# One level of seven products (quarter sums) in most of a feed-forward's first product, on one Trainium2 core

## The chip, the core and the metric

The kernel runs on one core of a Trainium2 chip: TensorE (matmuls), VectorE (DVE), ScalarE (ACT), GpSimd (POOL) and the DMA queues, issued here by SyncE (SP). The metric is the device time of one execution in microseconds; lower is better.

## The reference, cut to what matters

Two transformer-like layers follow each other on 512 tokens of width 1024. The change touches the very last stage, the feed-forward of the second layer:

```python
def sqrelu_mlp(h, w1, w2):
    a = jax.nn.relu(h @ w1)        # h 512 x 1024, w1 1024 x 4096
    return (a * a) @ w2            # w2 4096 x 1024
...
x = x + g2 * sqrelu_mlp(hx2, w_mlp1[l], w_mlp2[l])
```

All operands are float32.

## The kernel before

Every float32 operand is split into a high part (a copy rounded to fp32r, by ACT) and a low part (the operand less its high part, by VectorE), and a product is the sum of three matmuls: high x high, high x low, low x high (`products`, L682).

The first product of the last feed-forward has 32 column blocks of 128 output columns (`MF` = 32, numbered from `M1_N`). A block's weights are 1024 x 128, held as 128 x 1024 in `RAW`, four slots loaded by SP; its high and low parts lie in `WH` and `WL`, two slots each. The transposed tokens are in `HH` and `HL`, 8 blocks of the inner dimension by 512 tokens. `column_block` (L692) runs 8 x 3 matmuls of 512 tokens into one bank of PSUM. Blocks 0 and 1 are done in token halves (`token_half`, L705), so that they can start before the last tokens are there. For each block ACT makes the high part (L1458) of the block two ahead, then a Relu out of PSUM into `CT` (L2115); VectorE makes the low part (L2145) and squares into `M1` (L2960). Blocks wait for each other by counting semaphores (`w_high`, `w_low`, `w_used`, `mlp_relu`, `mlp_out`); a load waits until the low part of its slot is made (L534). GpSimd has nothing to do in this stage.

The second product (`down`, from `M2_N`) takes the 32 blocks of `M1` as stationary operands against rows of `w_mlp2`, which VectorE first multiplies by a gate row (`gate`, L2151). It has the same pace: 24 matmuls of 512 for each block. In other stages GpSimd works at elementwise additions and products, where VectorE is busy too; those rows are used below.

Of the kernel before, what the change touches and what calls it, by code (L numbers as in the profile page):

```python
# [8 lines left out]
F32 = mybir.dt.float32  # L9
F32R = mybir.dt.float32r  # L10
# [5 lines left out]
P = 128  # L16
T = 512
# [132 lines left out]
M1_ = 4096  # L150

# [53 lines left out]
def program(nc, a, laid, cst, dft, gmod, gcum, gpad, gexp, moved, out):  # L205
# [9 lines left out]
    with ctx:  # L215
# [4 lines left out]

        def sem(name):
            if name not in S:
                S[name] = ctx.enter_context(nc.semaphore(name))
            return S[name]

# [18 lines left out]
        sb("arena_front", [P, 10240])  # L244
        FHW = sb("last_high", [P, 4, D], F32R)
        FLW = sb("last_low", [P, 4, D], F32R)
        sb("arena_middle", [P, 6144])
        XL = sb("context_low", [P, KD, CTX], F32R)
        sb("arena_rest", [P, ARENA - 26624])
# [264 lines left out]

        def each(v, n):

            return v.unsqueeze(1).to_broadcast([P, n, v.shape[1]])
# [10 lines left out]
        def _(sp):  # L528
# [134 lines left out]
            blocks(sp, MF, columns(M1_N, 0, mlp1_v))  # L663
            blocks(sp, MF, rows(M2_N, a["w_mlp2_2"][0]))
# [16 lines left out]
        def _(pe):  # L681
            def products(out_, wh, wl, xh, xl, start, stop):  # L682


                pe.matmul(out_, wh, xh, start=start, stop=False)  # L685
                pe.matmul(out_, wh, xl, start=False, stop=False)  # L686
                return pe.matmul(out_, wl, xh, start=False, stop=stop)  # L687
# [744 lines left out]
            def mlp(g, j):  # L1432
                pe.wait_ge(sem("mlp_out"), 4 * g + j + 1)
                column_block(g, M1_N + j, j, HH, HL)

            for j in range(2, 4):
                mlp(0, j)
            with pe.Fori(1, MF // 4) as g:
                for j in range(4):
                    mlp(g, j)  # L1440
            down(M2_N, M2_A, MF, lambda t, m: m.then_inc(sem("rows_done"), 1) if t == NT - 1 else None,
                 lambda t: pe.wait_ge(sem("mlp_relu"), MF - 2 if t == 0 else MF))
# [3 lines left out]
        def _(act):  # L1446
# [658 lines left out]
            def mlp(g, j):  # L2105
                last = isinstance(g, int) and g == MF // 4 - 1 and j == 3
                if last:
                    for i in range(2):
                        act.wait_ge(sem("mlp_out"), 4 + i + 1)
                        act_split(0, i, M2_A, M2_N, arena(M1_, MF, T))  # L2110
# [12 lines left out]
        def _(dve):  # L2123
# [824 lines left out]
            def mlp(g, j):  # L2948
                last = isinstance(g, int) and g == MF // 4 - 1
                if last and j == 1:  # L2950
                    dve.wait_ge(sem("wb_in"), 48)
                if last and j > 0:
                    gate(M2_N + j - 1, WB)
                if last and j == 3:
                    for i in range(2):
                        act_split(0, i, M2_A, M1)
# [219 lines left out]
```

## Time and profile before

| what | value |
|---|---|
| median of the runs (1599.33 to 1599.58) | 1599.55 us |
| span of the profiled execution | 1597.8 us |
| TensorE busy | 1578.1 us, 99% |
| VectorE busy | 960.2 us, 60% |
| ACT busy | 676.3 us, 42% |
| GpSimd busy | 170.3 us, 11% |

The page has the busy share of each engine and the chain that ended last; further views give the groups of instructions, who waited for whom, and instructions in order of time. Matmuls overlap each other in their durations, so their pace is read from start times.

### The profile page before, as it was taken

The page shows a single profiled execution, that of the slowest core. Times are in us where ns is not written, and L with a number is a line of the kernel's source. Part 1 is how long each engine was busy: PE and PEld are TensorE (multiplying, and loading weights), DVE is VectorE, ACT ScalarE, POOL GpSimd, SP SyncE. Part 2 cuts the span into 40 slices and gives each one's busy share as a digit, 9 for nine tenths or more (in the row PEclk, how much of TensorE's full clock was granted, in tenths as well). Part 3 has the DMA queues.
Part 4 walks back from the last instruction along what each step waited for, and adds up shares of the span by engine and source line. Part 5 has one row for each costly group of instructions (what it writes and reads, how often), then busy time and mean ns, then how long its engine had stood idle before and what let it go on. Part 6 is the DMA issues. An engine that isn't in the chain of part 4 may idle for free.

```text
span 1597.8 us, 21438 instructions
## 1 busy us (share of the span) xinstructions
PE 1578.1 (99%) x8269; PEld 1299.1 (81%) x8269; DVE 960.2 (60%) x1435; ACT 676.3 (42%) x1178; POOL 170.3 (11%) x191
## 2 busy tenths in 40 slices
PE   9999999999999999999999999999999999999998
PEld 7878878789887877788888788877888888888886
DVE  5688867947545877776435448655577433355554
ACT  5464466555334333344334354544444422332321
POOL 2012134601001000000001132320000000000000
PEclk9999999999999999999999999999999999999999
DMA  7365243311354886532323133221223233323222
GB/s 201 93 166 126 80 107 78 89 47 39 132 197 145 280 286 227 188 100 92 115 92 119 42 96 86 67 72 55 80 80 119 80 92 103 93 95 103 92 95 77
DMA packets 198569, 180.67 MB, mean 113 GB/s; under 512 B 6078, under 2 KB 178189, under 8 KB 195412
## 3 DMA queue, kind: packets, MB, share of 16 engines
q1 hardware_dynamic: 195056, 171.13, 35.0%
q10 hardware_dynamic: 2276, 6.95, 1.3%
q0 software_dynamic: 1152, 1.44, 0.5%
q8 instruction: 56, 0.92, 0.2%
q14 instruction: 29, 0.24, 0.0%
HBM read 175.15 MB, written 4.58 MB: 112 GB/s over the span
## 4 chain that ended last, share of the span: by engine, by line
PE 92%; DVE 4%; ACT 2%; issue 1%; DMA 0%; POOL 0%; ACTq 0%; DVEq 0%; POOLq 0%
PE acc L685 17%; PE acc L686 16%; PE acc L687 16%; PE acc L728 7%; PE acc L729 7%; PE acc L730 7%; PE acc L1233 2%; PE acc L743 2%; PE acc L741 2%; PE acc L1235 2%; PE acc L1234 2%; PE acc L742 2%; PE acc L1377 1%; PE acc L1361 1%; DVE w_low L2145 1%
## 5 line engine op out<-in xcount | busy, mean ns | idle before, releaser
L2145 DVE TENSOR_TENSOR w_low<-w_raw,w_high 128x1024 fp32r<-128x1024 f32 x230 | 284.6, 1239 | 486.3 <-ACT w_high L1458 485.8
L1458 ACT ACTIVATE w_high<-w_raw 128x1024 fp32r<-128x1024 f32 x224 | 237.4, 1060 | 618.8 <-PE acc L687 367.9
L685 PE MATMUL acc<-h_high,w_high 128*128 128x512 f32 (+1 forms) x1248 | 487.2, 390 | 4.6 <-DVE h_low L2179 1.6
L687 PE MATMUL acc<-h_high,w_low 128*128 128x512 f32 (+1 forms) x1248 | 479.4, 384 | 0.0
L686 PE MATMUL acc<-h_low,w_high 128*128 128x512 f32 (+1 forms) x1248 | 479.2, 384 | 0.0
L685 PEld LDWEIGHTS acc<-h_high,w_high 128*128 128x128 f32 x1248 | 234.6, 188 | 64.0 <-issue 15.3
L687 PEld LDWEIGHTS acc<-h_high,w_low 128*128 128x128 f32 x1248 | 234.5, 188 | 47.1
L686 PEld LDWEIGHTS acc<-h_low,w_high 128*128 128x128 f32 x1248 | 234.7, 188 | 45.0 <-issue 1.2
L728 PE MATMUL acc<-w_high,act_high 128*128 128x512 f32 x496 | 193.3, 390 | 0.9 <-DVE arena L2671 0.6
L730 PE MATMUL acc<-w_high,act_low 128*128 128x512 f32 x496 | 193.0, 389 | 0.0
L729 PE MATMUL acc<-w_low,act_high 128*128 128x512 f32 x496 | 193.0, 389 | 0.0
L728 PEld LDWEIGHTS acc<-w_high,act_high 128*128 128x128 f32 x496 | 93.1, 188 | 21.0 <-DVE arena L2671 1.0
L730 PEld LDWEIGHTS acc<-w_high,act_low 128*128 128x128 f32 x496 | 93.1, 188 | 19.5
L729 PEld LDWEIGHTS acc<-w_low,act_high 128*128 128x128 f32 x496 | 93.1, 188 | 19.1
L2270 DVE SCALAR_TENSOR_TENSOR arena<-acc,conv_params,arena 128x511 f32<-128x511 f32 (+2 forms) x108 | 80.6, 746 | 2.5
L2662 DVE SCALAR_TENSOR_TENSOR arena<-acc,params,arena 128x511 f32<-128x511 f32 x88 | 65.7, 746 | 1.5
L2159 DVE TENSOR_TENSOR act_low<-arena,act_high 128x512 fp32r<-128x512 f32 x78 | 53.0, 685 | 10.7 <-ACT act_high L1466 10.7
L1466 ACT ACTIVATE act_high<-arena 128x512 fp32r<-128x512 f32 x78 | 47.9, 621 | 22.9 <-PE acc L730 19.1
L2151 DVE TENSOR_TENSOR w_raw<-w_raw,arena 128x1024 f32<-128x1024 f32 x40 | 48.7, 1218 | 0.0
L2984 POOL TENSOR_SCALAR small<-small 128x1 f32<-128x1 f32 x17 | 4.1, 239 | 378.7 <-ACT arena L1485 378.7
L2021 ACT ACTIVATE arena<-acc,small 128x512 f32<-128x512 f32 x32 | 21.7, 685 | 49.0 <-DVE small L2830 49.0
L1233 PE MATMUL acc<-w_high,h_high 128*128 128x512 f32 x96 | 37.7, 392 | 1.6 <-DVE h_low L2205 1.1
(392 smaller groups left out, 1955.7 us busy)
## 6 DMA issues: line engine op xcount, KB each, us to landing
w_raw<-w_in SPq DMA_DIRECT2D x68, 512.0 KB, 4.0
w_raw<-w_mlp SPq DMA_DIRECT2D x64, 512.0 KB, 3.9
w_raw<-w_up SPq DMA_DIRECT2D x44, 512.0 KB, 4.0
arena<-w_ada SPq DMA_DIRECT2D x13, 1024.0 KB, 7.9
w_raw<-w_out SPq DMA_DIRECT2D x24, 512.0 KB, 3.2
early<-w_ada SPq DMA_DIRECT2D x11, 1024.0 KB, 6.0
w_raw<-w_down SPq DMA_DIRECT2D x22, 512.0 KB, 3.2
w_raw<-w_branch_gate SPq DMA_DIRECT2D x16, 512.0 KB, 4.1
```

What stands on the lines that cost most here:

```text
L685: pe.matmul(out_, wh, xh, start=start, stop=False)
L686: pe.matmul(out_, wh, xl, start=False, stop=False)
L687: return pe.matmul(out_, wl, xh, start=False, stop=stop)
L728: pe.matmul(o, AH[:, r, tc], WH[:, s, fc], start=k_is_0, stop=False)
L729: pe.matmul(o, AH[:, r, tc], WL[:, s, fc], start=False, stop=False)
L730: m = pe.matmul(o, AL[:, r, tc], WH[:, s, fc], start=False, stop=False)
L1233: pe.matmul(o, xh, WH[:, n % 2, wc], start=k == 0, stop=False)
L1458: f(WH[:, off % 2, :], RAW[:, off % 4, :], ACT.Copy).then_inc(sem("w_high"), 1)
L2145: tt(WL[:, off % 2, :], RAW[:, off % 4, :], WH[:, off % 2, :].bitcast(F32), ALU.subtract).then_inc(sem("w_low"), 1)
L2159: tt(AL[:, r, :], src[:, 4 * g + j, :], AH[:, r, :].bitcast(F32), ALU.subtract)\
L2270: stt(tap(n)[:, lag:T], PS[:, conv_bank(n), 0:T - lag], CW[:, at:at + 1], tap(n)[:, lag:T], ALU.mult, ALU.add).then_inc(sem("conv_step"), 1)
L2662: stt(o, PS[:, ffn_bank(q, j), 0:T - lag], w, o, ALU.mult, ALU.add).then_inc(sem("ffn_step"), 1)
```

## The change

`WHOLE` = 6 blocks keep the old form. The other 26 form 13 pairs, and each pair (256 output columns x 512 tokens, inner dimension 1024) is computed as a 2 x 2 by 2 x 2 block product with seven instead of eight products of halves (Winograd's form of Strassen's method). A pair's weights are four quarters of 128 x 512. GpSimd's `first_sums` adds quarters 0+2 and 3+2; VectorE's `second_sum` and `fourth_sum` give two more. Sums of the token quarters are made once (`token_sums`, `token_high`, `token_low`). Each of the seven parts is 4 x 3 matmuls of 256 tokens (`part` on TensorE); its high (`part_high`, ACT) and low (`part_low`, VectorE) are made five parts ahead into a ring of six places, four in `WH`/`WL` and two in `AH`/`AL`. The results are combined by one copy (`keep_first`, ACT) and five VectorE operations of 256 elements (`second_part` to `second_quarter`), followed by Relus on ACT. The squares of a pair are one GpSimd operation of 1024 elements. Before the pairs, blocks 0 to 5 now write the Relu directly into `M1`. The loads of the last pairs and of the second product's first four rows wait for counts of `part_low`. The names that begin with `st_` are semaphores of earlier stages used again (`since` adds their old final count). `TOK0`, `TOK12` and `SUM31` lie over memory of the arena that is free by then; `second_sum` and `fourth_sum` write over raw quarters.

```diff
@@ -148,6 +148,8 @@
 AG_, AP_, APT_ = F_, F_ + 3072, F_ + 5120
 MT_ = 6144
 M1_ = 4096
+WHOLE, PAIRS = 6, 13
+RAWT_, TOK_, SUM_ = M1_ + 20 * T, (20480, 23552, 25600), 27648
...
+        def first_of(p):
+            return M1_N + WHOLE + 2 * p
+        def quarters(p):
+            at = first_of(p) % 4 * 1024
+            return RAW[:, :, :].rearrange("p a b -> p (a b)")[:, at:at + 2048].rearrange("p (q c) -> p q c", c=512)
+        SUM31 = arena(SUM_, 2, 512)
+        def operand(p, i):
+            q = quarters(p)
+            return [q[:, 0, :], q[:, 2, :], SUM31[:, 0, :], SUM31[:, 1, :], q[:, 3, :], q[:, 1, :], q[:, 0, :]][i]
+        def ring(s):
+            at = (s + 5) % 6
+            if at < 4:
+                c = slice(at % 2 * 512, at % 2 * 512 + 512)
+                return WH[:, at // 2, c], WL[:, at // 2, c]
+            return AH[:, at - 4, :], AL[:, at - 4, :]
+        def raw_tokens(i):
+            return arena(RAWT_ + 1024 * i, 4, 256)
+        def tokens(i):
+            if i < 3:
+                both = TOK12[:, i - 1] if i else TOK0[:, :, :, :]
+                return both[:, 0], both[:, 1]
+            return HH[:, 0:4, 256:512], HL[:, 0:4, 256:512]
+        def moving(i):
+            if i in (0, 5, 6):
+                k, tc = slice(0, 4) if i == 0 else slice(4, 8), slice(256, 512) if i == 6 else slice(0, 256)
+                return HH[:, k, tc], HL[:, k, tc]
+            return tokens([1, 2, 0, 3][i - 1])
+        def region(p, i):
+            bank, half = [(0, 0), (1, 0), (2, 0), (3, 0), (1, 256), (0, 0), (3, 0)][i]
+            return PS[:, 4 * ((p + 1) % 2) + bank, half:half + 256]
+        V1, V2, V3 = PAR[:, 0:2, :].rearrange("p a b -> p (a b)"), C1[:, 0:256], C1[:, 256:512]
+        def pair_out(p, first, n):
+            at = M1_ + (WHOLE + 2 * p) * T + first
+            return A[:, at:at + n]
...
-            blocks(sp, MF, columns(M1_N, 0, mlp1_v))
-            blocks(sp, MF, rows(M2_N, a["w_mlp2_2"][0]))
+            for j in range(WHOLE + 4):
+                columns(M1_N, 0, mlp1_v)(j // 4, j % 4)
+            def load_late(n, read, src, shape):
+                sp.wait_ge(sem("st_low"), since("st_low", read))
+                dst = RAW[:, n % 4, :]
+                if shape is not None:
+                    dst = dst.rearrange("p (k c) -> p k c", c=shape)
+                sp.dma_start(dst, src).then_inc(sem(f"w_in{n % 4}"), 16)
+            for p in range(2, PAIRS):
+                for e in range(2):
+                    j = WHOLE + 2 * p + e
+                    load_late(M1_N + j, 7 * (p - 2) + [7, 5][e], mlp1_v[:, :, j * P:(j + 1) * P], P)
+            w_mlp2 = a["w_mlp2_2"][0].rearrange("(k p) n -> k p n", p=P)
+            for j in range(4):
+                load_late(M2_N + j, 7 * (PAIRS - 2 + j // 2) + [7, 5][j % 2], w_mlp2[j], None)
+            with sp.Fori(1, MF // 4) as g:
+                for j in range(4):
+                    rows(M2_N, a["w_mlp2_2"][0])(g, j)
...
+            def part(p, i):
+                s = 7 * p + i
+                pe.wait_ge(sem("st_low"), since("st_low", s + 1))
+                if i == 0 and p == 1:
+                    pe.wait_ge(sem("mlp_relu"), WHOLE)
+                elif i == 0 and p > 1:
+                    pe.wait_ge(sem("st_read"), since("st_read", 2 * p - 3))
+                    pe.wait_ge(sem("st_out"), since("st_out", 5 * (p - 1)))
+                if p == 0 and 0 < i < 5:
+                    pe.wait_ge(sem("st_token_low"), since("st_token_low", [2, 3, 3, 4][i - 1]))
+                if i == 4:
+                    pe.wait_ge(sem("st_out"), since("st_out", 5 * p + 1))
+                elif i == 5:
+                    pe.wait_ge(sem("st_kept"), since("st_kept", p + 1))
+                elif i == 6:
+                    pe.wait_ge(sem("st_out"), since("st_out", 5 * p + 3))
+                o, (wh, wl), (xh, xl) = region(p, i), ring(s), moving(i)
+                for k in range(4):
+                    c = slice(k * P, (k + 1) * P)
+                    m = products(o, wh[:, c], wl[:, c], xh[:, k, :], xl[:, k, :], k == 0 and i < 5, k == 3, skip=i > 4)
+                if s == 7 * PAIRS - 1:
+                    m.then_inc(sem("w_used"), 2 * PAIRS)
+                else:
+                    m.then_inc(sem("st_done"), 1)
+            for p in range(PAIRS):
+                for i in range(7):
+                    part(p, i)
+            def pairs_read(t):
...
+            def token_high(i):
+                act.wait_ge(sem("st_tokens"), since("st_tokens", max(3, i + 1)))
+                if i == 3:
+                    used(0, M1_N + WHOLE - 1)
+                f(tokens(i)[0], raw_tokens(i), ACT.Copy).then_inc(sem("st_token_high"), 1)
+            def part_high(s):
+                p, i = divmod(s, 7)
+                if i in (0, 5):
+                    act.wait_ge(sem(f"w_in{first_of(p) % 4}"), 16 * (first_of(p) // 4 + 1))
+                elif i == 4:
+                    act.wait_ge(sem(f"w_in{first_of(p) % 4 + 1}"), 16 * (first_of(p) // 4 + 1))
+                elif i == 1:
+                    act.wait_ge(sem("st_sums"), since("st_sums", 2 * p + 1))
+                elif i == 6:
+                    act.wait_ge(sem("st_sums"), since("st_sums", 2 * p + 2))
                 else:
-                    split(g, M1_N + j + 2)
-                used(g, M1_N + j)
-                act.wait_ge(sem("mlp_out"), 4 * g + j + 3)
-                f(CT[:, j % 2, :], PS[:, j, :], ACT.Relu).then_inc(sem("mlp_relu"), 1)
-
-            blocks(act, MF, mlp, whole=1)
-            split(0, M2_N + 1)
-            down(M2_N, M2_A, MF, arena(M1_, MF, T), lambda m: act.wait_ge(sem("mlp_out"), MF + 4))
+                    act.wait_ge(sem("st_first"), since("st_first", p + 1))
+                if s > 5:
+                    act.wait_ge(sem("st_done"), since("st_done", s - 5))
+                else:
+                    used(0, M1_N + [-1, 4, 4, 5, 5, -1][s])
+                f(ring(s)[0], operand(p, i), ACT.Copy).then_inc(sem("st_high"), 1)
+            def keep_first(p):
+                act.wait_ge(sem("st_done"), since("st_done", 7 * p + 1))
+                if p:
+                    act.wait_ge(sem("st_out"), since("st_out", 5 * p - 4))
+                f(V1, region(p, 0), ACT.Copy).then_inc(sem("st_kept"), 1)
+            def first_quarter(p):
+                act.wait_ge(sem("st_done"), since("st_done", 7 * p + 6))
+                f(pair_out(p, 0, 256), region(p, 0), ACT.Relu).then_inc(sem("st_read"), 1)
+            def other_quarters(p):
+                act.wait_ge(sem("st_out"), since("st_out", 5 * p + 5))
+                f(pair_out(p, 256, 768), pair_out(p, 256, 768), ACT.Relu).then_inc(sem("st_read"), 1)
...
+            for s in range(7 * PAIRS):
+                p, i = divmod(s, 7)
+                if s + 5 < 7 * PAIRS:
+                    part_high(s + 5)
+                if s + 5 == 7 * PAIRS - 1:
+                    act.sem_inc(sem("w_high"), 2 * PAIRS)
+                if i == 6:
+                    first_quarter(p)
+                if i == 1:
+                    keep_first(p)
+                    if p:
+                        other_quarters(p - 1)
+                if s == 7 * PAIRS - 4:
+                    for j in range(2):
+                        act.wait_ge(sem("mlp_out"), 4 + j + 1)
+                        f(AH[:, (M2_A + j) % 4, :], M1[:, j, :], ACT.Copy).then_inc(sem("a_high"), 1)
+                if s == 7 * PAIRS - 3:
+                    gated_high(0, 7 * PAIRS - 4)
+                if s == 7 * PAIRS - 1:
+                    gated_high(1, 7 * PAIRS - 2)
+            other_quarters(PAIRS - 1)
...
+            def second_sum(p):
+                q = quarters(p)
+                dve.wait_ge(sem("st_first"), since("st_first", p + 1))
+                tt(q[:, 2, :], SUM31[:, 1, :], q[:, 0, :], ALU.add).then_inc(sem("st_sums"), 1)
+            def fourth_sum(p):
+                q = quarters(p)
+                dve.wait_ge(sem("st_sums"), since("st_sums", 2 * p + 1))
+                tt(q[:, 0, :], q[:, 2, :], q[:, 1, :], ALU.add).then_inc(sem("st_sums"), 1)
+            def part_low(s):
+                dve.wait_ge(sem("st_high"), since("st_high", s + 1))
+                h, l = ring(s)
+                tt(l, operand(*divmod(s, 7)), h.bitcast(F32), ALU.subtract).then_inc(sem("st_low"), 1)
+            def second_part(p):
+                dve.wait_ge(sem("st_done"), since("st_done", 7 * p + 2))
+                dve.wait_ge(sem("st_kept"), since("st_kept", p + 1))
+                if p:
+                    dve.wait_ge(sem("st_out"), since("st_out", 5 * p))
+                tt(V2, region(p, 1), V1, ALU.subtract).then_inc(sem("st_out"), 1)
+            def third_part(p):
+                dve.wait_ge(sem("st_done"), since("st_done", 7 * p + 3))
+                dve.wait_ge(sem("st_out"), since("st_out", 5 * p + 1))
+                tt(V3, V2, region(p, 2), ALU.subtract).then_inc(sem("st_out"), 1)
+            def last_quarter(p):
+                dve.wait_ge(sem("st_done"), since("st_done", 7 * p + 4))
+                dve.wait_ge(sem("st_out"), since("st_out", 5 * p + 2))
+                tt(pair_out(p, 768, 256), V3, region(p, 3), ALU.subtract).then_inc(sem("st_out"), 1)
+            def third_quarter(p):
+                dve.wait_ge(sem("st_done"), since("st_done", 7 * p + 5))
+                tt(pair_out(p, 512, 256), V3, region(p, 4), ALU.subtract).then_inc(sem("st_out"), 1)
+            def second_quarter(p):
+                if p == PAIRS - 1:
+                    dve.wait_ge(sem("w_used"), M2_N + 2)
                 else:
-                    split(g, M1_N + j + 2)
-                dve.wait_ge(sem("mlp_relu"), 4 * g + j + 1)
-                tt(M1[:, 4 * g + j, :], CT[:, j % 2, :], CT[:, j % 2, :], ALU.mult)\
-                    .then_inc(sem("mlp_out"), 1)
-
-            blocks(dve, MF, mlp, whole=1)
+                    dve.wait_ge(sem("st_done"), since("st_done", 7 * p + 7))
+                tt(pair_out(p, 256, 256), region(p, 6), V2, ALU.subtract).then_inc(sem("st_out"), 1)
...
+            split(0, M1_N + 2)
+            split(0, M1_N + 3)
+            token_sums()
+            square(0)
+            split(0, M1_N + 4)
+            square(1)
+            for i in range(3):
+                token_low(i)
+            split(0, M1_N + 5)
+            square(2)
+            part_low(0)
+            second_sum(0)
+            square(3)
+            square(4)
+            part_low(1)
+            part_low(2)
+            square(5)
+            part_low(3)
+            token_low(3)
+            part_low(4)
+            fourth_sum(0)
+            dve.sem_inc(sem("w_low"), 2 * PAIRS)
+            for s in range(7 * PAIRS):
+                p, i = divmod(s, 7)
+                if i == 0 and p:
+                    second_quarter(p - 1)
+                if i > 1 and i < 6:
+                    [second_part, third_part, last_quarter, third_quarter][i - 2](p)
+                if s + 5 < 7 * PAIRS:
+                    part_low(s + 5)
+                if i == 1 and p + 1 < PAIRS:
+                    second_sum(p + 1)
+                if i == 6 and p + 1 < PAIRS:
+                    fourth_sum(p + 1)
+                if p == PAIRS - 1:
+                    if i == 2:
+                        dve.wait_ge(sem("wb_in"), 48)
+                        gate(M2_N, WB)
+                    elif i == 3:
+                        gate(M2_N + 1, WB)
+                    elif i == 4:
+                        for j in range(2):
+                            act_split(0, j, M2_A, M1)
+                    elif i == 5:
+                        split(0, M2_N)
+                    elif i == 6:
+                        gate(M2_N + 2, WB)
+            second_quarter(PAIRS - 1)
...
+            def first_sums(p):
+                q = quarters(p)
+                for e in range(2):
+                    pool.wait_ge(sem(f"w_in{first_of(p) % 4 + e}"), 16 * (first_of(p) // 4 + 1))
+                if p:
+                    pool.wait_ge(sem("st_low"), since("st_low", 7 * (p - 1) + 4))
+                pool.tensor_tensor(SUM31, q[:, 0:4:3, :], each(q[:, 2, :], 2), ALU.add).then_inc(sem("st_first"), 1)
+            def squares(p):
+                pool.wait_ge(sem("st_read"), since("st_read", 2 * p + 2))
+                o = pair_out(p, 0, 1024)
+                pool.tensor_tensor(o, o, o, ALU.mult).then_inc(sem("st_square"), 1)
+            first_sums(0)
+            first_sums(1)
+            for p in range(PAIRS):
+                if p + 2 < PAIRS:
+                    first_sums(p + 2)
+                squares(p)
```

`token_sums` on VectorE is four operations of 1024 elements with two SBUF inputs; the fourth waits for the second, the second for the first. `token_low(i)` is one of 1024. In `down`'s first block TensorE waits for the last pairs' reads of PSUM (`pairs_read`).

## Rows read from the trace of the kernel before

**Rows 1.** The page: span, busy time, chain that ended last by engine
```profile
span 1597.8 us, 21438 instructions
...
PE 1578.1 (99%) x8269; PEld 1299.1 (81%) x8269; DVE 960.2 (60%) x1435; ACT 676.3 (42%) x1178; POOL 170.3 (11%) x191
...
PE 92%; DVE 4%; ACT 2%; issue 1%; DMA 0%; POOL 0%; ACTq 0%; DVEq 0%; POOLq 0%
```
**Rows 2.** Waits, 1254 to 1418: waiter <- releaser: us in total, times, longest
```profile
ACT w_high L1458 <- PE acc L687: 114.4, 30, 4.0
DVE w_low L2145 <- ACT w_high L1458: 108.4, 31, 4.8
```
**Rows 3.** Stretch: us, busy (instructions) by engine, granted clock, DMA share, GB/s
```profile
1254.37:1417.60 163.23, 163.23 (x723) 135.19 (x721) 59.56 (x66) 47.40 (x62) 0.00 (x0) 1.00 0.34 100
```
**Rows 4.** Timeline of TensorE: start us, us, engine, line, out<-in; block 2, second product
```profile
1254.37 0.40 PE L685 MATMUL acc<-h_high,w_high 128*128 128x512 f32 x1
...
1417.60 0.39 PE L728 MATMUL acc<-w_high,act_high 128*128 128x512 f32 x1
```
**Rows 5.** Timeline of TensorE: a matmul of 256 columns, 66 before 1254.37
```profile
1246.45 0.28 PE L685 MATMUL acc<-h_high,w_high 128*128 128x256 f32 x1
```
**Rows 6.** Timeline of VectorE, queued operations; the last has an input in PSUM
```profile
1414.65 0.69 DVE L2960 TENSOR_TENSOR arena<-arena 128x512 f32<-128x512 f32 x1
1415.25 1.22 DVE L2151 TENSOR_TENSOR w_raw<-w_raw,arena 128x1024 f32<-128x1024 f32 x1
1416.39 1.29 DVE L2159 TENSOR_TENSOR act_low<-arena,act_high 128x512 fp32r<-128x512 f32 x2
...
1011.34 0.42 DVE L2787 TENSOR_TENSOR arena<-arena,acc 128x255 f32<-128x255 f32 x1
```
**Rows 7.** Groups by form, 1250 to 1598, of ACT: xcount, busy us, mean ns
```profile
L1458 ACT ACTIVATE w_high<-w_raw 128x1024 fp32r<-128x1024 f32 x58 | 61.5, 1060 | 218.6 <-PE acc L687 118.8 <-PE acc L730 99.9
...
L1466 ACT ACTIVATE act_high<-arena 128x512 fp32r<-128x512 f32 x32 | 19.7, 620 | 4.3 <-PE acc L730 4.3
```
**Rows 8.** Single lines of GpSimd: ns min/median/max
```profile
L3023 POOL TENSOR_TENSOR arena<-arena,early x4: 2399/2411/2415, 105.0 to 181.2; 128x1024 f32<-128x1024 f32 x4
...
L3027 POOL TENSOR_TENSOR arena<-arena,small x3: 1909/1912/2953, 107.4 to 154.6; 128x1024 f32<-128x1024 f32 x3
```
**Rows 9.** Timelines of GpSimd and VectorE together; L2671 is a form's ns min/median/max
```profile
251.50 1.27 POOL L3048 TENSOR_TENSOR early<-early,masks 128x512 f32<-128x512 f32 x1
252.35 1.51 DVE L2145 TENSOR_TENSOR w_low<-w_raw,w_high 128x1024 fp32r<-128x1024 f32 x1 [0.86 <-ACT w_high L1458]
252.74 2.02 POOL L3046 TENSOR_TENSOR early<-early,small 128x512 f32<-128x512 f32 x1
...
1011.29 2.50 POOL L3134 TENSOR_TENSOR arena<-masks,arena 128x256 f32<-128x256 f32 x3 [21.01 <-PE acc L1280]
1011.67 0.83 DVE L2793 TENSOR_TENSOR act_low<-arena,act_high 128x448 fp32r<-128x448 f32 x1
1013.10 1.17 DVE L2793 TENSOR_TENSOR act_low<-arena,act_high 128x448 fp32r<-128x448 f32 x1
...
L2671 DVE TENSOR_TENSOR arena<-arena x22: 616/618/620, 526.1 to 763.2; 128x448 f32<-128x448 f32 x22
...
143.32 1.23 DVE L2330 TENSOR_TENSOR arena<-acc,arena 128x1024 f32<-128x1024 f32 x1
143.36 1.91 POOL L3032 TENSOR_TENSOR arena<-arena,small 128x1024 f32<-128x1024 f32 x1 [16.15 <-PE acc L880]
```
**Rows 10.** Timeline of VectorE: low part of block 3
```profile
1255.67 1.23 DVE L2145 TENSOR_TENSOR w_low<-w_raw,w_high 128x1024 fp32r<-128x1024 f32 x1 [1.06 <-ACT w_high L1458]
```
**Rows 11.** DMA issues on the page: xcount, KB each, median us to landing
```profile
w_raw<-w_mlp SPq DMA_DIRECT2D x64, 512.0 KB, 3.9
...
arena<-w_ada SPq DMA_DIRECT2D x13, 1024.0 KB, 7.9
```
**Rows 12.** Waits of TensorE over the whole span, the longest
```profile
PE acc L685 <- DVE h_low L2179: 1.6, 1, 1.6
```

More of the change, by code:

```diff
@@ L224, in sem, with since @@
             return S[name]
+        def since(name, n):
+            return ended[name][1] + n
         WH = sb("w_high", [P, 2, 1024], F32R)
@@ L681, in _, with products @@
         def _(pe):
[L682 to L687, printed above, removed]
+            def products(out_, wh, wl, xh, xl, start, stop, skip=False):
+                pe.matmul(out_, wh, xh, start=start, stop=False, skip_group_check=skip)
+                pe.matmul(out_, wh, xl, start=False, stop=False, skip_group_check=skip)
+                return pe.matmul(out_, wl, xh, start=False, stop=stop, skip_group_check=skip)
             def split_ready(g, off):
@@ L1430, in _ @@
             token_half(M1_N + 1, 1, 1, range(KD)).then_inc(sem("w_used"), 1)
[L1432 to L1442, printed above, removed]
+            for j in range(2, WHOLE):
+                if j > 3:
+                    pe.wait_ge(sem("mlp_relu"), j - 3)
+                column_block(0, M1_N + j, j % 4, HH, HL)
@@ L2117, in _, with relu @@
[L2117 to L2119 removed]
+            M1 = arena(M1_, MF, T)
+            def relu(j):
+                used(0, M1_N + j)
+                f(M1[:, j, :], PS[:, j % 4, :], ACT.Relu).then_inc(sem("mlp_relu"), 1)
+            def token_high(i):
[3 more added lines that the diff above has]
+                f(tokens(i)[0], raw_tokens(i), ACT.Copy).then_inc(sem("st_token_high"), 1)
@@ new lines, in _, with gated_high @@
+            split(0, M1_N + 2)
+            relu(0)
+            split(0, M1_N + 3)
+            relu(1)
+            for i in range(3):
+                token_high(i)
+            split(0, M1_N + 4)
+            relu(2)
+            split(0, M1_N + 5)
+            part_high(0)
+            relu(3)
+            relu(4)
+            part_high(1)
+            part_high(2)
+            relu(5)
+            part_high(3)
+            token_high(3)
+            part_high(4)
+            def gated_high(j, done):
+                n = M2_N + j
+                act.wait_ge(sem("w_gated"), gated_before(0, n))
+                act.wait_ge(sem("st_done"), since("st_done", done))
+                f(WH[:, n % 2, :], RAW[:, n % 4, :], ACT.Copy).then_inc(sem("w_high"), 1)
@@ L2122, in _, with squared @@
+            other_quarters(PAIRS - 1)
+            def squared(m):
+                if m < WHOLE:
+                    act.wait_ge(sem("mlp_out"), 4 + m + 1)
+                else:
+                    act.wait_ge(sem("st_square"), since("st_square", (m - WHOLE) // 2 + 1))
+            down(M2_N, M2_A, MF, M1, squared)
         @block.vector
@@ new lines, in token_low @@
+            def token_low(i):
+                dve.wait_ge(sem("st_token_high"), since("st_token_high", i + 1))
+                h, l = tokens(i)
+                tt(l, raw_tokens(i), h.bitcast(F32), ALU.subtract).then_inc(sem("st_token_low"), 1)
+            def second_sum(p):
[6 more added lines that the diff above has]
+                tt(q[:, 0, :], q[:, 2, :], q[:, 1, :], ALU.add).then_inc(sem("st_sums"), 1)
@@ new lines, in _ @@
+            split(0, M1_N + 2)
+            split(0, M1_N + 3)
+            token_sums()
+            square(0)
+            split(0, M1_N + 4)
+            square(1)
+            for i in range(3):
+                token_low(i)
+            split(0, M1_N + 5)
+            square(2)
[8 more added lines that the diff above has]
+            token_low(3)
```

55 lines of the change are left out of this document (34 added, 21 removed).

## The prediction

> **What bounds the kernel now.** I read the page first: TensorE is busy for 99% of the span and makes 92% of the chain that ended last [rows 1]. A busy matmul engine is no proof by itself, so the second view is the list of waits for the stretch of the changed product: ACT waits 114 us for TensorE and VectorE 108 us for ACT, and no row has TensorE wait [rows 2]. The stretch table says the same: 163.23 us, TensorE busy in all of it at a granted clock of 1.00 (its upper level, 2.4 GHz), VectorE in 59.6 us, ACT in 47.4, GpSimd in none [rows 3]. Third, the pace of the matmuls by start times, since their durations overlap. The first of the 30 whole column blocks starts at 1254.37 and the second product at 1417.60 [rows 4]: 163.23 / (30 x 24) = 0.2267 us for a matmul of 512 columns. So this stage is set by the number of matmuls times their pace, and a change that issues less matmul work gains until another engine becomes the slowest. The profiled span is 1597.8 us; the median is 1599.55, so 1.75 us lie around the span.
>
> **TensorE's part of the change.** A pair of column blocks took 2 x 24 matmuls of 512 columns: 48 x 0.2267 = 10.88 us. It becomes 7 parts of 4 x 3 matmuls of 256 columns, 84 in all. That is 7/8 of the columns in 1.75 times the instructions, so the pace of the short ones matters. The trace has 96 of them, in the two token-halved blocks: from 1246.45 to 1254.37 there are 66 steps [rows 4, 5], 0.120 us each. A part takes 12 x 0.120 = 1.44 us, a pair 10.08. Gain: 0.80 us a pair, 13 pairs, **10.4 us**. Each short matmul costs 13 ns over 256/2.4; that fixed piece, paid 84 times for 48, takes back 0.48 of the 1.36 us that 1/8 of a pair is.
>
> **VectorE's part.** Before, a pair asked VectorE for two low parts of 128x1024 and two squares of 128x512. Starts of queued operations lie 1.14 us apart for 1024 elements; an operation of 512 takes 0.69 and the next follows 0.60 after its start; 255 elements with an input in PSUM are followed at 0.33 [rows 6, 9]. Before: 2 x 1.14 + 2 x 0.60 = 3.5 us of each 10.88. After, for a pair: seven `part_low` and two sums (`second_sum`, `fourth_sum`), nine operations of 512 elements with both inputs in SBUF, 9 x 0.60 = 5.45; and five combinations of 256 with one input in PSUM, 5 x 0.34 = 1.70. **7.15 us**, which fits under 10.08. The squares go to GpSimd. ACT gets seven highs (0.62 at 512 elements), one copy and two Relus (each at most the 1.06 of 1024 elements) [rows 7]: at most 7.5 us a pair, with room.
>
> **GpSimd's part, and the lock.** For a pair GpSimd runs `first_sums` and `squares`, each 1024 elements with two SBUF inputs. The same form, one input repeated over a middle dimension, took 2.41 us (L3023); with a small operand 1.91 (L3027) [rows 8]. Taken alone 4.8 us, hidden. But the trace shows what happens when both engines read SBUF. At 252.35 a VectorE low part of 1.23 us takes 1.51 while the GpSimd operation from 251.50 to 252.77 is under way: it ends at 253.86, 1.09 after that one's end. The GpSimd operation behind it then takes 2.02 for the 1.27 of its neighbour: it waits for the VectorE one. One of the three of L3027 took 2.95 for 1.91 [rows 8]. From 1011.29 on, three GpSimd additions of 256 elements meet a queue of VectorE operations and the engines alternate: two of VectorE's, of 448 elements, take 0.83 and 1.17 where 0.62 is usual. The operation at 143.32 with an input in PSUM kept its 1.23 beside a GpSimd operation that kept its 1.91 [rows 9]. I read this as: a VectorE operation with two SBUF inputs and a GpSimd operation never run together, the second waits for the whole of the first, and a queue of VectorE operations does not keep GpSimd out.
>
> The Trainium skill says the same ("SBUF — State Buffer", "SBUF: two separate sides": the pair of ports that VectorE and GpSimd share is an exclusive lock and the later one "fully blocks"; "Who interferes with whom" adds that a VectorE instruction with two SBUF inputs is among those, one with at most one is not). By that rule the two engines' times add; the trace agrees, with 1.51 for 1.23 and 2.95 for 1.91. GPSIMD Engine Reference, "Elementwise — side-by-side cycle accounting", has 4497 ns for 2048 elements of a two-input add; an estimate from it is 2.25 us for 1024, and no more than the row's 2.41 would follow.
>
> So for a pair VectorE is occupied 7.15 us and barred for 2 x 2.33 (2.41 less the 0.08 that neighbours overlap): **11.8 us**, above TensorE's 10.08 and above the old 10.88. May the five PSUM operations run inside the barred time? In the order written out: `squares` is let go by ACT's Relu of 768 elements after `second_quarter`, 0.95 us on, while VectorE has two `part_low` (1.2 us) to do; GpSimd gets in behind these, and next in VectorE's queue is `second_sum`, two SBUF inputs. `first_sums(p+2)` is let go by `part_low` in step 5; GpSimd gets in one operation later, and next is `fourth_sum`. So nothing overlaps by my reading; at best one PSUM operation does at each (0.34). VectorE's lag reaches TensorE because part 4 overwrites the bank that `second_part` reads: TensorE waits there, with its later parts queued behind.
>
> **Start.** Block 3 ends at 1254.37 + 2 x 5.44 = 1265.25. VectorE ends the split of block 3 at 1256.9 [rows 10], then does four token sums of 1024 (4.8 us; the third ends at 1260.5). ACT makes three token highs (1.06 each [rows 7], to 1263.7) ahead of block 4's high, VectorE its low at 1266.0: 0.8 us of gap. Block 5 comes just in time: 0.6 + 3 x 1.14 + 1.14 on VectorE inside 5.44. It ends at 1276.9; Relu and square of block 5 to 1278.3, `part_low(3)` to 1278.9; now GpSimd's `first_sums(1)` is free and bars VectorE to 1281.3; `token_low(3)` to 1282.4, five operations of 0.60 and `second_part` to 1285.8. Part 4 could have started at 1276.9 + 4 x 1.44 = 1282.7: 3.1 us. Together 3.9.
>
> **Transfers.** The 26 loads of 512 KB keep their count; two are now asked back to back. One lands in 3.9 us, and a single 1 MB in 7.9 [rows 11]. From the release to the step that needs `first_sums` there is more than a whole pair, and 7.9 + 2.4 = 10.3 fits into 11.8, nothing. **End.** The last pair adds three gates, two low parts of activations and a split on VectorE (7 us), but has no lows for a next pair and no first sums; VectorE ends the split of the second product's first block about 0.5 us before TensorE is done. `first_sums` has no work from pair 11 on, so the long period counts between the fourth parts of pairs 0 and 11. The second product keeps its order, nothing; without that cover the late split would cost up to 1.1.
>
> **The sum.** -10.4 (TensorE) + 3.9 (start) + 11 x (11.8 - 10.08) = 18.9 gives +12.4. Span 1610.2, with 1.75 around it **1612.0 us**. Bounds of the period: 10.08 if everything hides; 7.15 + 2 x 1.83 - 2 x 0.34 = 10.13 with both GpSimd operations at the short form's price and a PSUM operation beside each; 7.15 + 4.16 - 0.34 = 10.97 with one short and one overlap; 9 x 0.69 + 5 x 0.42 + 2 x 2.41 = 13.1 if no neighbours overlap at all. I take 11.8, since L3023 is nearest in form. Each 0.1 us of the period is 1.1 us of the time.
>
> **Rivals.** (a) The sums and squares hide: VectorE idles in each period while it waits for TensorE's parts (10.08 - 7.15 = 2.9 us), and GpSimd slips in there. For it: VectorE's work alone fits. Against: 4.66 of bar do not fit into 2.9 without the overlaps of the second bound. It decides below a period of 10.67, where 11 x (10.67 - 10.08) = 6.5 = 10.4 - 3.9. Time at 10.08: 1599.55 - 10.4 + 3.9 = 1593. This is the one that ends faster. (b) Half hidden: period 10.97, 1602.9. (c) The hand-overs cost more (waits of semaphores at each step, ACT's high late by one): period 12.55, 1620. (d) Short matmuls do not keep 0.120 between parts, or the granted clock falls to its lower level after the gaps of 1.7 us that I expect on TensorE: the longest wait of TensorE in the trace is 1.6 us [rows 12], with no price seen. TensorE has 1.7 us of slack in each period, so this adds nothing before it exceeds that; with a fall after the 3.1 us gap some parts run at double, 1.44 us each, and two give 1615.
>
> **How the numbers follow.** Main case, period 11.4 to 12.2 (1607.6 to 1616.4): 0.50. Half hidden, period 10.8 to 11.4: 0.15, nearly all slower by over 0.2% (1602.8). Near break-even: 0.07. Hidden, faster by over 0.2% (below 1596.4): 0.16. Dearer, (c) and (d): 0.12. About 0.2% is what a measurement of this kernel can tell from no change. Slower 0.50 + 0.12 + 0.13 = 0.75, same 0.09, faster 0.16. The range 1599 to 1620 leaves out the hidden case and the dear tail.
>
> **What will tell.** Starts of TensorE's short matmuls at 0.120 with a gap of some 1.7 us before part 4 of most pairs, ended by VectorE's `second_part`; VectorE operations of 512 elements that take about 3 us instead of 0.69, twice a pair, each beside a GpSimd operation; VectorE's five PSUM operations untouched; GpSimd's at 2.4 plus up to 0.6. I am wrong if the slow operations of VectorE do not show, if the pair's period stands at 10.1, or if the gaps on TensorE end by ACT or a transfer.

## The result and the profile after

The changed kernel takes 1607.18 us (median of four runs, 1603.91 to 1610.22) against 1599.55: ratio 1.0048, 95% interval 1.0034 to 1.0061. The profiled execution is the one of 1603.91 us; its span is 1602.1, 4.3 us above the one of before. So 3.3 us of the 7.6 between the medians are not in this profile; experiment 5 comes back to them.

The page of the changed kernel, beside [rows 1]: span, busy time, chain by engine.

```profile
span 1602.1 us, 22455 instructions
...
PE 1573.0 (98%) x8737; PEld 1315.2 (82%) x8737; DVE 1060.1 (66%) x1573; ACT 711.2 (44%) x1260; POOL 232.4 (15%) x217
...
PE 89%; DVE 7%; ACT 2%; issue 1%; POOL 0%; ACTq 0%; DVEq 0%
```

The waits of TensorE in the stretch 1240 to 1440 (us in total, times, longest), and the stretch itself, beside [rows 3] (columns as there):

```profile
PE acc L787 <- DVE masks L3223: 8.6, 4, 3.6
```
```profile
1254.20:1421.70 167.50, 157.25 (x1190) 150.36 (x1188) 157.96 (x204) 83.22 (x145) 60.59 (x25) 0.99 0.34 95
```

L3223 is `second_part`. TensorE, which waited for nobody, now waits for it, and VectorE counts as busy in 158 of 167.5 us where its own work is 13 x 7.15 and the start. Its durations tell where that comes from. First a pair as most are, on GpSimd, VectorE and ACT (timeline; L3490 is `first_sums`, L3496 `squares`, L3209 `fourth_sum`, L3248 `second_quarter`, L3203 `second_sum`, L3215 the low parts):

```profile
1357.38 2.61 POOL L3490 TENSOR_TENSOR arena<-w_raw 128x1024 f32<-128x1024 f32 x1 [3.61 <-DMA w_raw<-w_mlp]
1357.65 2.89 DVE L3209 TENSOR_TENSOR w_raw<-w_raw 128x512 f32<-128x512 f32 x1
1360.46 0.41 DVE L3248 TENSOR_TENSOR arena<-acc,masks 128x256 f32<-128x256 f32 x1
1360.57 0.63 ACT L2269 ACTIVATE w_high<-w_raw 128x512 fp32r<-128x512 f32 x1 [2.44 <-DVE w_raw L3209]
...
1361.37 0.84 ACT L2286 ACTIVATE arena<-arena 128x768 f32<-128x768 f32 x1
...
1362.00 0.68 DVE L3203 TENSOR_TENSOR w_raw<-arena,w_raw 128x512 f32<-128x512 f32 x1
1362.29 2.14 POOL L3496 TENSOR_TENSOR arena<-arena 128x1024 f32<-128x1024 f32 x1 [2.30 <-ACT arena L2286]
1362.60 0.41 DVE L3223 TENSOR_TENSOR masks<-acc,params 128x256 f32<-128x256 f32 x1
1362.93 2.04 DVE L3215 TENSOR_TENSOR w_low<-w_raw,w_high 128x512 fp32r<-128x512 f32 x1
```

`fourth_sum` takes 2.89 us where 0.68 is its own: it begins behind GpSimd's operation and ends 0.6 after that one's end (1357.38 + 2.61 = 1359.99, 1357.65 + 2.89 = 1360.54). `second_part`, one input in PSUM, runs in its 0.41 inside `squares`; the low part behind it waits and takes 2.04. Then a pair of the long kind:

```profile
1326.51 2.41 POOL L3490 TENSOR_TENSOR arena<-w_raw 128x1024 f32<-128x1024 f32 x1 [7.94 <-DMA w_raw<-w_mlp]
1326.95 2.52 DVE L3215 TENSOR_TENSOR w_low<-w_raw,w_high 128x512 fp32r<-128x512 f32 x1 [0.65 <-ACT w_high L2269]
1328.88 2.34 POOL L3496 TENSOR_TENSOR arena<-arena 128x1024 f32<-128x1024 f32 x1
1329.39 2.38 DVE L3203 TENSOR_TENSOR w_raw<-arena,w_raw 128x512 f32<-128x512 f32 x1
1331.69 0.41 DVE L3223 TENSOR_TENSOR masks<-acc,params 128x256 f32<-128x256 f32 x1
1332.25 0.36 PE L787 MATMUL acc<-h_high,w_high 128*128 128x256 f32 x1 [1.81 <-DVE masks L3223]
```

Here `first_sums` is released late, by the landing of its load, `squares` is ready when it ends, and both bar VectorE ahead of `second_part`. TensorE waits 1.81 us. Three pairs after the first are of this kind, with periods (start of part 4 to the next) of 12.0 us and more; four of the others have 10.53 to 10.66, and those behind a long one 10.08 to 10.17 us.

### The profile page after: what moved, and what is told of

Same layout as the page of the kernel before. It is cut to its first block, busy times and chain, and to the rows that moved or that the text cites. A ratio compares the mean times of both kernels' runs of the same rounds, so it can differ in the third digit from the quotient of the medians.

```text
span 1602.1 us, 22455 instructions
## 1 busy us (share of the span) xinstructions
PE 1573.0 (98%) x8737; PEld 1315.2 (82%) x8737; DVE 1060.1 (66%) x1573; ACT 711.2 (44%) x1260; POOL 232.4 (15%) x217
## 3 DMA queue, kind: packets, MB, share of 16 engines
q0 software_dynamic: 1152, 1.44, 0.5%
## 4 chain that ended last, share of the span: by engine, by line
PE 89%; DVE 7%; ACT 2%; issue 1%; POOL 0%; ACTq 0%; DVEq 0%
PE acc L787 16%; PE acc L789 15%; PE acc L788 15%; PE acc L830 7%; PE acc L831 7%; PE acc L832 7%; PE acc L1335 2%; PE acc L1337 2%; PE acc L843 2%; PE acc L1336 2%; PE acc L845 2%; PE acc L844 2%; DVE w_low L2369 1%; PE acc L1479 1%; PE acc L1463 1%
## 5 line engine op out<-in xcount | busy, mean ns | idle before, releaser
L2369 DVE TENSOR_TENSOR w_low<-w_raw,w_high 128x1024 fp32r<-128x1024 f32 x204 | 252.4, 1238 | 382.8 <-ACT w_high L1591 382.3
L787 PE MATMUL acc<-h_high,w_high 128*128 128x512 f32 (+1 forms) x1172 | 444.7, 379 | 14.2 <-DVE masks L3223 8.6
L789 PE MATMUL acc<-h_high,w_low 128*128 128x512 f32 (+1 forms) x1172 | 436.0, 372 | 0.0
L788 PE MATMUL acc<-h_low,w_high 128*128 128x512 f32 (+1 forms) x1172 | 435.8, 372 | 0.0
L1591 ACT ACTIVATE w_high<-w_raw 128x1024 fp32r<-128x1024 f32 x196 | 207.7, 1060 | 506.2 <-PE acc L789 251.9
L787 PEld LDWEIGHTS acc<-h_high,w_high 128*128 128x128 f32 x1172 | 220.8, 188 | 67.7 <-issue 27.2
L789 PEld LDWEIGHTS acc<-h_high,w_low 128*128 128x128 f32 x1172 | 220.8, 188 | 38.6
L788 PEld LDWEIGHTS acc<-h_low,w_high 128*128 128x128 f32 x1172 | 221.0, 189 | 37.4 <-issue 1.2
L3215 DVE TENSOR_TENSOR w_low<-w_raw,w_high 128x512 fp32r<-128x512 f32 x42 | 47.2, 1132 | 2.8 <-ACT w_high L2269 2.8
L3490 POOL TENSOR_TENSOR arena<-w_raw 128x1024 f32<-128x1024 f32 x13 | 33.7, 2589 | 88.2 <-DMA w_raw<-w_mlp 60.1
```

The lines of the kernel that those rows point to most:

```text
L787: pe.matmul(out_, wh, xh, start=start, stop=False, skip_group_check=skip)
L788: pe.matmul(out_, wh, xl, start=False, stop=False, skip_group_check=skip)
L789: return pe.matmul(out_, wl, xh, start=False, stop=stop, skip_group_check=skip)
L1591: f(WH[:, off % 2, :], RAW[:, off % 4, :], ACT.Copy).then_inc(sem("w_high"), 1)
L2369: tt(WL[:, off % 2, :], RAW[:, off % 4, :], WH[:, off % 2, :].bitcast(F32), ALU.subtract).then_inc(sem("w_low"), 1)
```

## The experiments

**1. GpSimd's work made short (e1).** Is it the length of GpSimd's operations, or the many hand-overs? This kernel leaves out most of the sums and squares, so only its time is read.

```diff
-                pool.tensor_tensor(SUM31, q[:, 0:4:3, :], each(q[:, 2, :], 2), ALU.add)...
+                pool.tensor_tensor(SUM31[:, :, 0:16], q[:, 0:4:3, 0:16], each(q[:, 2, 0:16], 2), ALU.add)...
-                pool.tensor_tensor(o, o, o, ALU.mult)...
+                pool.tensor_tensor(o[:, 0:32], o[:, 0:32], o[:, 0:32], ALU.mult)...
```

> The changed kernel with GpSimd's two operations of a pair cut to 16 and 32 elements each, all waits and counts kept; the rest of the sums and squares is left out, so only the time is read. Theory 1, VectorE is barred while GpSimd reads: nothing bars it now, VectorE needs 7.15 us of 10.08, no gap before part 4 in any pair but the first, period 10.08; the first gap falls from 3.6 to about 1.3 us, so 1599.55 - 10.4 + 0.8 (gap at block 4) + 1.3 = 1591 us. Theory 2, the hand-overs between engines (waits at each step, ACT one step late) make the gaps and the length of GpSimd's work does not matter: it stays at 1604 to 1607.

Measured 1590.67 us, ratio 0.9946 (0.9931 to 0.9961). With the same waits and the same number of instructions, TensorE's waits for `second_part` shrink to one, in the first pair:

```profile
PE acc L787 <- DVE masks L3223: 1.5, 1, 1.5
```

The period is 10.02 us, so with this kernel's waits the hand-overs cost nothing that can be seen; the 16.5 us between it and the changed one come with the length of GpSimd's two operations. Of the 13.3 us between the two profiled executions, 2.1 are the shorter first gap (1.46 for 3.60 us) and 1.5 a lower clock behind that gap, which this run does not have (last section); nearly all the rest is the period.

**2. Squares on ACT, then the sums on VectorE too (e2, e3).** Both compute everything.

```diff
 e2, in other_quarters on ACT:
+                act.wait_ge(sem("st_read"), since("st_read", 2 * p + 2))
+                f(pair_out(p, 0, 1024), pair_out(p, 0, 1024), ACT.Square).then_inc(sem("st_square"), 1)
 e3, as e2, and in second_sum on VectorE:
+                for e in range(2):
+                    dve.wait_ge(sem(f"w_in{first_of(p) % 4 + e}"), 16 * (first_of(p) // 4 + 1))
+                tt(SUM31, q[:, 0:4:3, :], each(q[:, 2, :], 2), ALU.add).then_inc(sem("st_first"), 1)
                 dve.wait_ge(sem("st_first"), since("st_first", p + 1))
```

> The squares of a pair go from GpSimd to ACT, after its Relu of 768 elements; GpSimd keeps the first sums. Theory 1 (barring): one bar of 2.33 us is left, VectorE 7.15 + 2.33 = 9.5 of 10.08, gaps before part 4 vanish except in the first pair (3.6 us, and some 1.3 us of lower clock after it): 1599.55 - 10.4 + 0.8 + 3.6 + 1.3 = 1595 us. ACT gets 1 us more a pair, 7 of 10.08. Theory 2 (hand-overs): ACT has one more step in its queue, so it stays at 1604 to 1607 or gets worse.

> Squares on ACT, and the first sums on VectorE right ahead of the second sum: GpSimd has nothing to do. Theory 1 (barring): the sum costs VectorE 1.14 us itself and saves a bar of 2.33; VectorE 8.4 of 10.08, no gaps but the first (2.4 us and some 0.9 of lower clock): 1599.55 - 10.4 + 0.8 + 2.4 + 0.9 = 1593 us, faster than e2 though VectorE has more work. Theory 2, VectorE's own amount of work and its order decide: slower than e2 by up to 1.1 us a pair.

Measured: e2 1594.91 us (ratio 0.9971, 0.9959 to 0.9983), e3 1591.97 us (0.9957, 0.9943 to 0.997). Taking `squares` off GpSimd gives 12.3 us; moving `first_sums` to VectorE gives 2.9 more although VectorE then has more to do. But most of it lies in the first pair. Of the 4.0 us between the two profiled executions 1.0 is its gap (2.62 us in e3, 3.60 in e2) and 2.4 the lower clock behind the longer one, which e3 does not have; the later periods differ by 0.6 us in sum, since one bar still fits under TensorE's pace. VectorE's groups in e3 (xcount, busy us, mean ns) show every operation at its own price again, and the sum at half of what it had barred; in e2 the first line of these had a mean of 978 ns:

```profile
L3220 DVE TENSOR_TENSOR w_low<-w_raw,w_high 128x512 fp32r<-128x512 f32 x42 | 28.8, 686 | 11.3 <-ACT w_high L2269 11.3
L3206 DVE TENSOR_TENSOR arena<-w_raw 128x1024 f32<-128x1024 f32 x13 | 15.8, 1218 | 0.0
```

In e3 part 4 of pair 0 starts at 1285.07 and that of pair 11 at 1395.34: a period of 110.27 / 11 = 10.02 us, TensorE's own pace (rows of its timeline).

**3. Everything on VectorE (e7).** As e3, with the squares as one VectorE operation in step 3 of the next pair.

> As e3, with the squares on VectorE too, GpSimd and ACT have none of the moved work. VectorE's own 7.15 + 1.24 + 1.14 = 9.5 us of 10.08, the same sum as in e2 where 2.33 of it was a bar. Theory 1 (only the sum on VectorE counts): no gaps but the first, 1592 to 1594 us. Theory 2 (at 94% the order of the steps already shows, since second_part waits behind the square): gaps of some tenths in each pair, 1595 to 1600.

Measured 1592.31 us (0.9961, 0.9945 to 0.9976). VectorE's 9.5 us still fit; TensorE waits only in the first pair. The two operations cost 2.4 us on the engine that seemed too full for them, and up to 4.7 us of the same engine's time (2 x 2.33, by the prediction's price) when they were given away; in an ordinary pair of the changed kernel 2.2 + 1.4 = 3.6.

**4. When the loads land (e4, e5).** The changed kernel with its loads released at another step of VectorE: in e4 both at least one step later, in e5 only the second of a pair, one step ahead of the first, behind which it was queued:

```diff
 e4:
-                    load_late(M1_N + j, 7 * (p - 2) + [7, 5][e], ...
+                    load_late(M1_N + j, 7 * (p - 2) + [8, 8][e], ...
 e5:
-                for e in range(2):
+                for e in (1, 0):
-                    load_late(M1_N + j, 7 * (p - 2) + [7, 5][e], ...
+                    load_late(M1_N + j, 7 * (p - 2) + [7, 6][e], ...
```

> The changed kernel, with each load of a pair's weights asked for one step of VectorE later (0.95 us or more). Theory A, the landing of the loads decides in which order GpSimd's two operations meet VectorE's queue: first_sums starts when its second load has landed; about 1.2 us later it runs into squares, both bar VectorE in one piece of 4.7 us ahead of second_part, and nearly every pair becomes one of 12 us instead of 10.65: 1599.55 - 10.4 + 5.7 (start, with the lower clock) + 11 x 1.9 = 1616 us, and little spread between runs. Theory B, the loads are hidden and the spread comes from elsewhere: 1604 to 1610 as before.

> The changed kernel, but a pair's second load is asked for first, one step earlier than the other (it had been queued behind that). Theory A (landing decides): first_sums starts as soon as part_low lets it go or shortly after, squares comes behind second_sum, and part of its bar lies over second_part, which reads PSUM: all pairs at about 10.7 us, none at 12: 1599.55 - 10.4 + 5.7 + 11 x 0.6 = 1601.5 us, spread under 2 us. Theory B: 1604 to 1610 with the spread as before.

Measured: e4 1621.82 us (1.0148, 1.0132 to 1.0163), e5 1601.01 us (1.0011, 1.0001 to 1.002), within 1600.61 to 1601.64. So the same work takes from 1601 to 1622 us by a step or two (about 1 us each) in the release of transfers. GpSimd in e4, then in e5 (timeline):

```profile
1355.92 2.41 POOL L3490 TENSOR_TENSOR arena<-w_raw 128x1024 f32<-128x1024 f32 x1 [7.41 <-DMA w_raw<-w_mlp]
1358.28 2.36 POOL L3496 TENSOR_TENSOR arena<-arena 128x1024 f32<-128x1024 f32 x1
1368.50 2.41 POOL L3490 TENSOR_TENSOR arena<-w_raw 128x1024 f32<-128x1024 f32 x1 [7.87 <-DMA w_raw<-w_mlp]
1370.95 2.26 POOL L3496 TENSOR_TENSOR arena<-arena 128x1024 f32<-128x1024 f32 x1
```
```profile
1354.70 2.69 POOL L3490 TENSOR_TENSOR arena<-w_raw 128x1024 f32<-128x1024 f32 x1 [3.52 <-DVE w_low L3215]
1359.70 2.14 POOL L3496 TENSOR_TENSOR arena<-arena 128x1024 f32<-128x1024 f32 x1 [2.30 <-ACT arena L2286]
1365.36 2.70 POOL L3490 TENSOR_TENSOR arena<-w_raw 128x1024 f32<-128x1024 f32 x1 [3.52 <-DVE act_low L3215]
1370.35 2.14 POOL L3496 TENSOR_TENSOR arena<-arena 128x1024 f32<-128x1024 f32 x1 [2.30 <-ACT arena L2286]
```

In e4 the two touch in nearly every pair, and TensorE waits for `second_part` in all pairs but one, 23.6 us in total; the periods are 12.1 to 13.2 us, longer than the 12 I had put, and the time is 6 us above my number. Two things that my sum left out show in its trace. TensorE's clock falls three more times, after the waits of pairs 3, 6 and 9, and the periods with these falls are the long ones, 13.18, 13.18 and 12.86 us, against 12.1 to 12.6 for the others after the first (13.17, with the fall behind the first gap). And between 1290 and 1420 VectorE stands idle 21 us in e4 for 5 in the changed kernel, 16.4 of them for highs of ACT and 4.6 for `first_sums`: a landing that is this late also costs by itself, and not only by the order. In e5 the landing no longer appears as a releaser from pair 3's `first_sums` on; the operations lie 5.0 us apart and the period is 10.65 (1359.70 to 1370.35). e5 has the first gap and the lower clock too and spreads over 1 us, so these two do not make the 6 us of spread of the changed kernel.

**5. The changed kernel once more (e9),** for another profile.

> The changed kernel once more, unchanged, for another profile of it, since its times spread over 6 us. Theory: a slower execution has more periods of 12 us, in which first_sums starts late (released by the landing) and squares follows it at once; each long period in place of a quiet one of 10.65 adds 1.4 us. The profile at 1603.9 us had three (before part 4 of pairs 3, 4 and 10) after the first gap. One of about 1607 us would have five or six, and one of 1610 seven or eight. Rival: the spread lies elsewhere (the first gap, the granted clock, the end) and the count of long periods stays at three.

Measured 1604.05 to 1609.76 us, median 1605.26. The profiled execution is again the fastest of its set, 1604.05, and has again three long periods after the first, now at pairs 3, 4 and 7 instead of 3, 4 and 10. All three `first_sums` are released by a landing there. That the long ones wander fits a transfer's landing; that a slower execution has more of them was not seen, since none was profiled.

**6. The start (e6, e8).** From e3 on. e6 changes the order in the first pair (block 4's high ahead of the token highs; `second_part`, `third_part`, `last_quarter` of pair 0 ahead of other work); e8 also squares blocks 0 to 5 on ACT:

```diff
 e6, on VectorE:
-            square(5)
             part_low(3)
             token_low(3)
             part_low(4)
+            second_part(0)
             fourth_sum(0)
+            square(5)
 e8, in relu(j) on ACT:
+                act.wait_ge(sem("mlp_relu"), j + 1)
+                f(M1[:, j, :], M1[:, j, :], ACT.Square).then_inc(sem("mlp_out"), 1)
```

> Without GpSimd (as e3), and the first pair's steps in another order: block 4's high ahead of the token highs on ACT; on VectorE second_part, third_part and last_quarter of pair 0 ahead of block 5's square, of low parts 6 and 7 and of second_sum(1). Theory: the gaps of 0.54 at block 4 and of 2.6 us before part 4 are order, not amount: both go, 1591.97 - 0.6 - 2.7 = 1588.7 us. Rival: the gap only moves to parts 5, 6 or to pair 1, since the work of VectorE in the start (some 18 us of it in 22) stays: 1590.5 to 1592.

> As e6, with the squares of blocks 0 to 5 on ACT too: VectorE has 6 x 0.60 = 3.6 us less to do in the start, ACT 6 x 0.6 more. Theory: in e6 the gap only moved to pair 1 (1.9 us before its part 4) since VectorE's amount of work in the start stayed; now it goes: 1591.65 - 2.1 = 1589.5 us. Rival: ACT's queue in the start, with each square behind a wait for its own Relu, holds up the highs of parts 0 to 4, and a gap of about the same size comes back: 1591 to 1592.

Measured: e6 1591.65 us (0.995, 0.9937 to 0.9964), no better than e3 beyond the spread; e8 1590.21 us (0.9941, 0.9927 to 0.9955). The waits of TensorE for `second_part` in e3, e6 and e8:

```profile
PE acc L787 <- DVE masks L3228: 2.6, 1, 2.6
```
```profile
PE acc L787 <- DVE masks L3229: 1.9, 1, 1.9
```
```profile
PE acc L787 <- DVE masks L3231: 1.5, 1, 1.5
```

In e6 the gap ends at 1293.80, before part 4 of pair 1 instead of pair 0: the rival of that run was right, the order had been less at fault than the amount. In e8 3.6 us less of VectorE's work took only 0.4 off that gap. The time still came within 0.7 us of my 1589.5, but not by that theory: the profiled executions differ by 0.74 us, the medians by 1.44, and where the rest comes from was not traced. In e8 VectorE's last pause before `second_part` of pair 1 is one of 0.70 us, to 1286.09, for a high that waited for that pair's `second_sum`; from there it works through its queue to 1292.83. Whether another order of that queue would close the gap stays open. e8 is the fastest version, 9.5 us under its runs of before and 15 to 17 under the changed kernel.

## Why the prediction was right, and where it was off

I forecast 1612.0 us, 1599 to 1620, slower with 0.75. The time is 1607.18.

- **What bounds it and the mechanism: right.** TensorE's new wait is for `second_part`, VectorE's operations with two SBUF inputs last up to 2.9 us beside GpSimd's, those with an input in PSUM keep 0.41, and e1 takes the whole loss away. Experiments 1 and 2 landed within about 1 us of what the same sum gave for them. The Trainium skill ("SBUF — State Buffer", "Who interferes with whom") has VectorE instructions with two SBUF inputs contend with GpSimd instructions that read SBUF, and those with at most one not. The trace agrees: 2.89 for 0.68 with both inputs in SBUF, 0.41 with one.
- **TensorE's gain: right, a little larger.** 0.120 us a matmul by my rows gave 10.08 a pair; e3 shows 10.02, since the parts with token sums take 1.42, so 0.857 x 13 = 11.1 us instead of 10.4. (The 0.48 us that the prediction takes back belongs to the 1.28 us of pure column time, not to 1.36; the 0.80 it ends with is right.)
- **The start: right in sum, one piece missing.** Part 4 of pair 0 starts at 1286.08 in the profile, for 1285.8 in the working; the sum is right because its two gaps are off in opposite directions, 0.4 for 0.8 us at block 4 and 3.6 for 3.1 before part 4. After this gap of 3.6 us the granted clock fell; I had named that only as a rival, with 0.12 for it and the dearer hand-overs together. It cost 1.5 us in this profile (below).
- **The period: the term that was mis-sized.** I took 11.8 us for all eleven. Part 4 of pair 11 starts at 1406.89: 120.81 / 11 = 10.98 (the first, 11.57, holds the 1.5 us of lower clock). That is the size of rival (b), half hidden, 10.97 with a chance of 0.15, and not of the main case, which began at 11.4. The step that failed is "GpSimd gets in behind these, and next in VectorE's queue is `second_sum`", 0.95 us after `second_quarter`. ACT's Relu of the 768 is queued behind the high of part 6, and that one waits for `fourth_sum`, which is itself barred (2.44 us of wait in the row at 1360.57). So `squares` comes at 1362.29, behind `second_sum`; `second_part` lies inside it, and the next low part pays 1.36 us instead of 2.33: 7.15 + 2.2 + 1.36 = 10.7, and 10.66 is measured (`squares` at 1351.63 and 1362.29). I had walked VectorE's queue in order, but not ACT's. In the three long pairs `squares` did come ahead of `second_sum`, as I had written. The price of `squares` was too high as well: it reads one tensor twice, and where VectorE did not keep it waiting it took 1.92 us, with the bar on the VectorE operation behind it, not the 2.41 of `first_sums`' form. Of the 0.97 us between 2.33 and 1.36 this is about 0.5, and `second_part` inside it 0.33 (an estimate from these rows).

```profile
1424.09 1.92 POOL L3496 TENSOR_TENSOR arena<-arena 128x1024 f32<-128x1024 f32 x1 [6.51 <-ACT arena L2286]
1424.18 2.91 DVE L2375 TENSOR_TENSOR w_raw<-w_raw,arena 128x1024 f32<-128x1024 f32 x1
```

- **Transfers: wrong as "nothing".** I counted whether the loads land in time for `second_sum` (they do) and not what their landing does to the place of `first_sums` in VectorE's queue. In the profile nine of its releases come from a landing. Three pairs have it late enough for a period of 12.0, 12.05 and 12.35; in two of them the landing released it, in the first (1313.42) the profile names a low part. Experiment 4 shows that the place of the landing is worth 1601 or 1622 us.
- **The sum with measured terms:** 11 x (11.8 - 10.98) = 9.0 us too much. Part 4 of pair 11 comes 8.7 us earlier than worked out, with 0.3 from the start the other way, and from there on ten parts and a wait of 0.3: the second product starts at 1421.71, I had 1430.0. With the 3.3 us between the profiled run and the median, that is 1612.0 against 1607.2. That the median lies so near the main case (from 1607.6) is in part luck: the 3.3 us stand in no profile, and the 1.5 us of lower clock stood in no term of the sum.

## What to carry to other kernels

In these runs GpSimd did not add to VectorE where VectorE's operations read two SBUF inputs: a 1024-element operation cost VectorE 1.14 us if it did it itself and 1.4 to 2.3 us of bar if GpSimd did it, so give such work to ACT or to VectorE, and keep GpSimd for times in which VectorE reads PSUM or is idle. Seven products for eight pay here, once the helper engines are kept apart: 1590.2 against 1599.7 us. When two engines exclude each other, walk every queue that releases their work, ACT's and the transfers' too: where they meet changed the time by 21 us with the same instructions. And gaps of about 2 us on TensorE in each pair cost more than their length once the clock falls, as in e4.

## What the runs showed of the hardware that I had not expected

With the first gap of 3.6 us (3.9 between starts) TensorE's clock fell to its lower level in all five profiles that have this gap: for 3.4 us in the changed kernel, e4 and e5, where the fall came about 1 us after TensorE had started again, and for 6.8 us in e2 and e9, where it came inside the gap. After a single gap of 1.5 to 2.6 us (e1, e3, e6, e7, e8) it stayed. But a shorter gap is not safe by itself: in e4, with 1.1 to 2.4 us of wait in each pair, it fell after three waits of 2.35, 1.88 and 1.98 us, for 3.4 us each time, and stayed after others of the same size; what decides between them these runs do not show. The columns are those of [rows 3]; first the changed kernel, then e3 in the same place, then e4 after its wait of 2.35 us:

```profile
1287.50:1290.50 3.00, 3.00 (x16) 3.00 (x16) 1.92 (x4) 0.63 (x1) 0.00 (x0) 0.50 0.98 266
```
```profile
1287.50:1290.50 3.00, 3.00 (x27) 3.00 (x26) 2.38 (x6) 1.54 (x3) 0.00 (x0) 1.00 0.10 27
```
```profile
1325.00:1328.00 3.00, 3.00 (x16) 3.00 (x15) 2.52 (x5) 0.63 (x1) 0.00 (x0) 0.50 0.66 181
```

A granted clock of 0.50 is 1.2 GHz; TensorE started 16 matmuls in such a stretch instead of 27. Parts 4 and 5 of pair 0 took 1.81 and 2.56 us for 1.44 each, 1.5 us lost; in e2 2.70 and 2.56, 2.4 us; after the later falls of e4 the two parts took 4.44 us together, 1.6 us lost each time.
